# One transpose and one small transfer for a row of maxima, maxima moved behind and between, and a reordered first front

## What is computed

```python
k_sh = head_rmsnorm(kvf[..., :D]); v_sh = kvf[..., D:2 * D]
c_all = jnp.cumsum(log_sigmoid(kvf[..., 2 * D:] + kv_f_bias), axis=1)
q = head_rmsnorm(proj[..., :D]); z = proj[..., D:]
logits = (q @ k.T) * HEAD_DIM ** -0.5 + c_q - c_k      # causal, per head
out = h + ((softmax(logits) @ v) * silu(z)) @ w_out
```

## Time and profile before

| what | us |
|---|---|
| median of 3 runs | 1886.25 (1883.72 to 1886.79) |
| the profiled execution | 1883.0 |
| its span | 1880.9 |
| PE busy in it | 1812.6 (96%) |
| DVE, ACT, POOL busy | 965.2, 945.8, 465.6 |

### The profile page before, as it was taken

The page is one execution under the profiler, slowest core; times in us unless marked ns, Lnnn a source line. Parts: engine busy times, 40 slices in busy tenths (PEclk is TensorE's granted clock), DMA queues, the critical chain, the costliest instruction groups (busy, mean ns, idle before and its releaser), DMA issues.

```text
span 1880.9 us, 55776 instructions
## 1 busy us (share of the span) xinstructions
PE 1812.6 (96%) x24247; PEld 1578.4 (84%) x24247; DVE 965.2 (51%) x1864; ACT 945.8 (50%) x1721; POOL 465.6 (25%) x464
## 2 busy tenths in 40 slices
PE   6899999999999999999899999999999999999998
PEld 5798989889898999899798888888888888887676
DVE  6456666666666666666533833443443344334421
ACT  6555454555545464555423645555455555554621
POOL 3323242423324242332500411212121212111000
PEclk9999999999999999999999999999999999999999
DMA  7101010100101010010342200111110111111334
GB/s 251 34 9 45 9 53 9 42 17 21 41 9 51 9 53 9 28 31 9 105 136 76 88 23 23 29 29 30 34 35 24 40 28 30 29 29 30 100 104 136
DMA packets 105362, 88.78 MB, mean 47 GB/s; under 512 B 4065, under 2 KB 96852, under 8 KB 104996
## 3 DMA queue, kind: packets, MB, share of 16 engines
q1 hardware_dynamic: 99400, 65.87, 12.1%
q0 software_dynamic: 2864, 12.34, 2.1%
q10 hardware_dynamic: 2860, 7.02, 1.1%
HBM read 64.43 MB, written 20.80 MB: 45 GB/s over the span
## 4 chain that ended last, share of the span: by engine, by line
PE 87%; DVE 5%; ACT 4%; issue 2%; POOL 1%; DMA 1%; SPq 0%; ACTq 0%; DVEq 0%
PE ps L2115 8%; PE ps L2752 7%; PE ps L2645 6%; PE ps L2116 6%; PE ps L2117 6%; PE ps L2646 6%; PE ps L2647 6%; PE ps L2028 3%; PE ps L2030 3%; PE ps L2029 3%; PE ps L2207 3%; PE ps L2226 3%; PE ps L2721 2%; PE ps L2694 2%; PE ps L2724 2%
## 5 line engine op out<-in xcount | busy, mean ns | idle before, releaser
L2115 PE MATMUL ps<-xh,wh 128*128 128x258 f32 (+1 forms) x1008 | 315.0, 313 | 3.6 <-ACT arena L1190 2.2
L2116 PE MATMUL ps<-xh,wl 128*128 128x258 f32 (+1 forms) x1008 | 286.3, 284 | 0.0
L2117 PE MATMUL ps<-xl,wh 128*128 128x258 f32 (+1 forms) x1008 | 286.2, 284 | 0.0
L2645 PE MATMUL ps<-xh,wh 128*128 128x348 f32 x744 | 253.7, 341 | 4.6 <-ACT arena_b L1446 3.8
L2646 PE MATMUL ps<-xh,wl 128*128 128x348 f32 x744 | 239.1, 321 | 0.0
L2647 PE MATMUL ps<-xl,wh 128*128 128x348 f32 x744 | 239.0, 321 | 0.0
L1973 DVE TENSOR_REDUCE arena_b<-ps 128x1 f32<-128x144 f32 (+4 forms) x224 | 106.5, 506 | 200.5 <-PE ps L2698 180.3
L2115 PEld LDWEIGHTS ps<-xh,wh 128*128 128x128 f32 x1008 | 190.3, 189 | 16.2 <-ACT arena L1190 3.6
L2116 PEld LDWEIGHTS ps<-xh,wl 128*128 128x128 f32 x1008 | 190.8, 189 | 2.0
L2117 PEld LDWEIGHTS ps<-xl,wh 128*128 128x128 f32 x1008 | 190.1, 189 | 0.0
L1149 ACT ACTIVATE arena<-ps,pp 128x257 f32<-128x257 f32 (+1 forms) x128 | 61.1, 478 | 225.6 <-PE ps L2117 225.6
(11 more groups left out here) (320 smaller groups left out, 4538.8 us busy)
## 6 DMA issues: line engine op xcount, KB each, us to landing
wr<-in_w_in SPq DMA_DIRECT2D x33, 512.0 KB, 4.5
wr<-in_kv_w SPq DMA_DIRECT2D x16, 512.0 KB, 4.0
wr<-in_b_w_in SPq DMA_DIRECT2D x16, 512.0 KB, 4.0
arena<-xt_scr SPq DMA_DIRECT2D x8, 522.0 KB, 4.4
xt_scr<-arena POOLq DMA_DIRECT2D x1, 4176.0 KB, 13.5
wr<-in_w_out SPq DMA_DIRECT2D x8, 512.0 KB, 4.2
ob_scr<-arena_b POOLq DMA_DIRECT2D x16, 256.0 KB, 2.9
wr<-in_b_w_out SPq DMA_DIRECT2D x8, 512.0 KB, 5.2
```

Of the source, the lines that this page charges most:

```text
L2115: pe.matmul(bank, wh[:, j, k, :], xh[:, k, t], start=(k == 0), stop=False)
L2116: pe.matmul(bank, wl[:, j, k, :], xh[:, k, t], start=False, stop=False)
L2117: mm = pe.matmul(bank, wh[:, j, k, :], xl[:, k, t], start=False, stop=(k == KO - 1))
L2645: pe.matmul(bank[:, 0:SEG], wh[:, slot, k, :], xh[:, k, t], start=(k == 0), stop=False)
```

## The change

- `maxrow`: PE makes one transpose of all 8 columns of `mcol` into 8 partitions of one bank; ACT copies it negated to a new tile `m_neg` (8 x 128), waits for that copy (`m_neg`), and issues a DMA that writes it as 1,024 values of one partition of `qb2`. The first scores wait for the DMA's semaphore, the users of the bank for `m_neg` alone.
- `order`: a new list `mid[g]` stands between `scores` of group g+1 and `weighted` of group g. Projection pieces are not interrupted any more; two maxima stand behind a piece, and up to two in `mid`.
- `first_round` has `maxrow` 0 ahead of the last half piece of z, and the last pair has `maxrow` 1 ahead of its `bo` step in fill 7.
- `FRONT_ONLY` begins with the k and v steps; r is whole ahead of `kks`. The copy and the shift of the third low-rank piece move into the step `low`.

```diff
@@ order @@
-                    fill[2] = m(2) + proj(0, 1, *m(2))
-                    fill[3] = m(2) + proj(0, 2, *m(2))
-                    fill[4] = ([("sumsq", 0, i) for i in range(3)] + [("den", 1), ("rsq", 0)] + proj(1, 0, *m(2)) + m(1))
-                    fill[5] = m(2) + proj(1, 1, *m(1)) + [("norm", 0)]
+                    fill[2] = proj(0, 1) + m(2)
+                    mid[2] = m(2)
+                    fill[3] = proj(0, 2) + m(2)
+                    mid[3] = m(2)
+                    fill[4] = [("sumsq", 0, i) for i in range(3)] + [("den", 1), ("rsq", 0)] + proj(1, 0) + m(2)
+                    mid[4] = m(1)
+                    fill[5] = proj(1, 1) + [("norm", 0)] + m(2)
+                    mid[5] = m(1)
...
-                    fill[7] = [("bo", 0, 2), ("maxrow", 1)]
+                    fill[7] = [("maxrow", 1), ("bo", 0, 2)]
...
-                fill[3] = [("vrow", 0, 0), ("vrow", 0, 1)] + m(2) + proj(3, 0, *m(2))
-                fill[4] = m(2) + proj(3, 1, *m(2)) + [("gated", 0)]
-                fill[5] = m(2) + [("proj", 3, 2, 0)] + m(2)
-                fill[6] = m(2) + [("wsplit",)]
+                fill[3] = [("vrow", 0, 0), ("vrow", 0, 1)] + proj(3, 0) + m(2)
+                mid[3] = m(2)
+                fill[4] = proj(3, 1) + [("gated", 0)] + m(2)
+                mid[4] = m(2)
+                fill[5] = [("proj", 3, 2, 0)] + m(2)
+                mid[5] = m(2)
+                fill[6] = [("wsplit",)] + m(2)
...
-                steps += [("weighted", e, g)]
+                steps += mid[g] + [("weighted", e, g)]
@@ first_round @@
-            return steps + maxima[10:] + z[5:] + [("maxrow", 0)]
+            return steps + maxima[10:] + [("maxrow", 0)] + z[5:]
@@ FRONT_ONLY @@
-        FRONT_ONLY = ([("low",), ("decay",), ("first", 3)] + FRONT_IN[0][1:] + sum(FRONT_IN[1:5], []) + FRONT_IN[5][:2]
-                      + [("rsqrt",)] + FRONT_IN[5][2:] + FRONT_IN[6])
+        FRONT_ONLY = ([("k", 2), ("v", 2), ("low",), ("decay",), ("first", 3), ("exps",), ("kraw",), ("tables",), ("r", 0),
+                       ("r", 1), ("r", 2), ("kks",)] + FRONT_IN[5][:2] + [("rsqrt",)] + FRONT_IN[5][2:] + FRONT_IN[6])
@@ ACT, ahead of the list and in low @@
-            act.wait_ge(S.lora_part, 3)
-            act.activation(mut_lo[:, 2 * SEG + 1:], G[0][:, 2, :], ACT.Copy, scale=param(C_LORA)).then_inc(S.mu_done, 1)
+            act.sem_inc(S.mu_done, 1)
...
+                        if begin:
+                            act.wait_ge(S.lora_part, 3)
+                            act.activation(mut_lo[:, 2 * SEG + 1:], G[0][:, 2, :], ACT.Copy, scale=param(C_LORA))\
+                                .then_inc(S.lora_mu, 1)
@@ DVE, the same @@
+                        if begin:
+                            dve.wait_ge(S.lora_mu, 3)
+                            dve.scalar_tensor_tensor(seg3(lo)[:, 2, :], G[0][:, 2, :], param(C_NLORA), lora_mut[:, 2, :],
+                                                     ALU.mult, ALU.add).then_inc(S.hi_part, 1)
@@ ACT, maxrow @@
-                        for a in range(2):
-                            act.wait_ge(S.m_row_done, 4 * q_ + 2 * e + a + 1)
-                            act.activation(qb2[e][HD:HD + 1, META + a * 512:META + (a + 1) * 512], ps[0:1, B_SM[a], :],
-                                           ACT.Copy, scale=-1.0).then_inc(S.m_row, 1)
+                        n_ = 2 * q_ + e
+                        act.wait_ge(S.m_row_done, n_ + 1)
+                        if n_:
+                            act.wait_ge(S.m_row, 16 * n_)
+                        act.activation(m_neg[:, :], ps[0:KO, B_SM[0], 0:P], ACT.Copy, scale=-1.0).then_inc(S.m_neg, 1)
+                        act.wait_ge(S.m_neg, n_ + 1)
+                        act.dma_start(f32(qb2[e][HD:HD + 1, META:T]), f32(m_neg[:, :])).then_inc(S.m_row, 16)
@@ PE, maxrow and scores @@
-                        for a in range(2):
-                            for t in range(4):
-                                mm = pe.transpose(ps[0:1, B_SM[a], t * P:(t + 1) * P], mcol[:, 4 * a + t:4 * a + t + 1],
-                                                  ident[:, :])
-                            mm.then_inc(S.m_row_done, 1)
+                        pe.transpose(ps[0:KO, B_SM[0], 0:P], mcol, ident[:, :]).then_inc(S.m_row_done, 1)
...
-                                pe.wait_ge(S.m_row, 4 * p + 2 * e + 2)
+                                pe.wait_ge(S.m_row, 16 * (2 * p + e + 1))
```

More of the change, by code:

```diff
@@ L208, in __init__ @@
         self.m_row = sem("m_row")
+        self.m_neg = sem("m_neg")
         self.st_done = sem("st_done")
@@ L262, in build @@
         params = sb("params", [P, NCOLS])
+        m_neg = sb("m_neg", [KO, P], F32R)
         pp = sb("pp", [P, NQ])
@@ L457, in m @@
                 return [next(maxima) for _ in range(n)]
-            fill = [[] for _ in GROUPS]
+            fill, mid = [[] for _ in GROUPS], [[] for _ in GROUPS]
             if e == 0:
@@ L1197, in round_act_a @@
                         if begin:
-                            act.wait_ge(S.shifted, 1)
+                            act.wait_ge(S.hi_part, 3)
                             act.activation(lo[0:LORA, SEG_T[0][1]:], lo[0:LORA, SEG_T[0][1]:], ACT.Tanh)\
@@ L1640, in _ @@
             dve.scalar_tensor_tensor(seg3(lo)[:, 1, :], G[0][:, 1, :], param(C_NLORA), lora_mut[:, 1, :], ALU.mult, ALU.add)
-            dve.wait_ge(S.mu_done, 1)
-            dve.scalar_tensor_tensor(seg3(lo)[:, 2, :], G[0][:, 2, :], param(C_NLORA), lora_mut[:, 2, :], ALU.mult,
-                                     ALU.add).then_inc(S.shifted, 1)
+            dve.sem_inc(S.shifted, 1)
             def split_row(r, k):
@@ L2600, in _ @@
                     if first and i < 2:
-                        pe.wait_ge(S.hi_part, i + 3)
+                        pe.wait_ge(S.hi_part, i + 4)
                     elif i == 0 or first:
@@ L2656, in round_pe @@
                             elif not first:
-                                pe.wait_ge(S.m_row, 4 * p + 4)
+                                pe.wait_ge(S.m_neg, 2 * p + 2)
                             elif j == 0:
@@ L2685, in round_pe @@
                             if not first:
-                                pe.wait_ge(S.m_row, 4 * q_ + 2 * e)
+                                pe.wait_ge(S.m_neg, 2 * q_ + e)
                         elif i >= 2:
@@ L2734, in round_pe @@
                             if m:
-                                pe.wait_ge(S.m_row, 4 * KO)
+                                pe.wait_ge(S.m_neg, 2 * KO)
                             else:
```

## The result

The change made the kernel slower: median 1903.97 us against 1886.47 us before (6 runs each), a ratio of 1.009 with a 95% interval of 1.0074 to 1.0106. The forecast was 1875 us. The profiled execution took 1899.9 us, 16.9 more than the one before.

What follows compares the result with a forecast made beforehand. PE, busy 96% of the span, was taken as the bound; -12.2 + 3.3 + 1.1 - 3.0 = -10.8 us from the median of 1886.25 gave 1875.4, stated as 1875. Range 1868 to 1883, leaving out rivals 2 and 3.

Steps and rivals of the forecast that it cites:

- Transposes, -12.2 us: In `maxrow`, one transpose replaces eight: 0.76 us saved 16 times, all on the path.
- The row's way: From transpose to first scores by copy and DMA: issue at +0.65, row there at +2.45, needed at +2.9; stall 0.
- The two bounds of 2.6 and 4.0 us: Slower landings of the row's DMA, from two other loads: row there at +3.25 or +4.65, stalls 0.35 or 1.75.
- The collision: At `maxrow`, SP's weight load comes 0.6 to 0.8 us earlier and overlaps the row's traffic; a few tenths lost, inside cover.
- Rival 2: Before the first scores, the row queues behind the weight load or lands at 4.0 us: +17 us, 1892; chance 0.07.
- Uncovered wait, +3.3 us: Second half of a pair: maxima no longer cover the z piece's wait for the v rows; 0.47 us over 7 pairs.
- Shortest group, +1.1 us: Maxima pairs around the shortest scores wait for DVE's reductions of two PSUM banks: 0.15 us over 7 pairs.
- First front, -3.0 us: Before the first mask: k and v steps earlier, r whole, z starts near 60.9 and ends at 66.0 instead of 69.0.
- Rivals 3 and 4: Maxima wait for DVE at 49 places, 1886, chance 0.09; the front gives nothing because of later waits, 1878, chance 0.1.

Runs made afterwards that it cites:

- row_only: Kernel before with only the new `maxrow` (one transpose, copy, DMA), maxima in their old places within `order`; 1875.58 us, ratio 0.9958.
- split_only: Changed kernel with only ACT's split of the next k weights moved behind the row of maxima; 1877.84 us, ratio 0.9951.
- cover_only: Changed kernel with only the first two maxima of a pair's second half put ahead of the z piece again; 1896.22 us, ratio 1.0049.
- wait_filled: cover_only with six repeats of a product, thrown away, ahead of PE's wait for head 0's row; 1884.77 us, ratio 0.9998.
- order_only: Kernel before with only the new fills and `mid`, the old `maxrow` kept; 1890.01 us, ratio 1.0029.

## Why the prediction was wrong

- *Transposes, -12.2 us*: right in mechanism, a tenth too large: 1.36 us per pair instead of 1.53. The whole of row_only is -9.6 us, with 1.5 us of waits in it.
- *The row's way*: the issue at +0.61 against +0.65, the landing alone at 1.8 us, as taken: in row_only and split_only PE uses the row 2.16 us after the issue without a wait, and at head 1 of the last pair, where its cover is shortest, at 1.84. The two bounds of 2.6 and 4.0 us were not needed for a transfer by itself.
- *The collision, "Eight small packets between 1024 should lose a few tenths, inside the cover"*: this is the step that failed. I had worked out that the load would come 0.6 to 0.8 us earlier against the row; it did (0.97 us behind the transpose before, 0.34 now). What I priced wrongly was the meeting. The row's packets did not go between the load's but behind them, which costs the row about 2 us: seven landings of 3.7 to 4.6 us after the issue instead of 1.8, +11.6 us of waits. Rival 2 had this mechanism and place, and its 1.75 us for one wait was near the 1.66 measured; but it counted nine places and more, 17 us, and seven came about: the first round has no load near its row, and head 1 of the last pair has none either. It got 0.07, and its time of 1892 was still 12 us short.
- The rule of the Trainium skill that I set beside rival 2 ("DMA: Bandwidth & Descriptors", the section on queues, rings and completion order: a DMA engine takes turns between queues packet by packet) was taken to make it a few tenths. In the trace the row's packets do not take turns with the load's: issued 0.27 us behind it, they ran at its end and the row landed in 3.8 us; 0.37 us ahead of it, PE had the row in 2.2, with one exception of 2.7. The section's packet holds several descriptors, typically 9 to 17 and at most 64; the load has 1,024 pieces of 512 B, an estimated 64 on each of 16 engines. So "packet by packet" leaves room for a wait of a whole load, which "a few tenths" left out. That the load was one packet on each engine is not shown, and the row in the middle of the load (0.16 us ahead) speaks against it.
- *The clock*: missing. I had the two gaps' own lengths in the sum or in the rivals and assumed the full level around them, though the trace before shows the level falling behind gaps in the front and in the last pair. Between cover_only and wait_filled it is 11.4 us, in the changed kernel 13 in the windows from 1180 to 1700 us alone. That is the largest single error, and why even rival 2 fell short.
- *Uncovered wait, +3.3 us*: right. 0.45 us per pair, 0.47 forecast. *Shortest group, +1.1 us*: 0.04 per pair instead of 0.15; nothing.
- *First front, -3.0 us*: -2.2 measured. The interval of its ratio reaches from -4.0 to -0.4 us, so the term stands. Its working has a slip: by its own rates, 24 products from 60.9 with the slow level until 65.2 end at 66.3, not 66.0, which gives -2.7.
- Rivals 3 and 4 did not come about: L2711 waits 3.9 us for DVE in the whole span against 5.1 before, and the front's gain stayed. (The 4.9 us before all lie in the last pair, none in the first round.)

Summed up again with what was measured: 1886.5 - 9.5 for the transposes - 2.2 + 3.3 + 11.6 + 13 gives 1902.7, against 1904.0. Part of that match is luck: the 13 us leave out the lower clock outside 1180 to 1700 us, and the terms count seven pairs, not all. The sum is better tested on the stretch of 649.2 us: -9.5 + 3.3 + 11.6, and 15.4 for ten falls of the clock of 1.54 us each (the price of one is worked out at the end), give +20.8 against 21.7 measured.

## What to carry to other kernels

- In a kernel bound by PE, price a wait by what it leaves in its neighbourhood: a gap of 1.1 to 1.7 us, harmless by itself, cost as much again through the clock here. Filling it with products that are thrown away was worth 11.4 us here; removing it is better.
- Here a small transfer with 2 us of cover was late whenever a large one was issued just ahead of it, or less than 0.2 us behind. Look at every queue's issues within 1 us of it after the change, not before it; here the remedy was to put ACT's copy, from which the load follows by way of GpSimd and SP, behind the row.
- Measure the parts alone when a change has several: -2.2, -9.6 and +4.9 us were each within 2.6 us of their forecast, and only their meeting gave +17.5.

## What the runs showed of the hardware that was not expected

- The issue of the row's DMA occupies ACT's queue for 0.63 to 0.66 us (8 rows of 512 B into one partition; the first two of a run took 1.26 and 0.7), against 0.23 us for the 8.2 KB load of two rows.
- The race is decided by 0.3 us or so: the row's DMA issued 0.37 us ahead of the load lands in time, 0.16 us ahead it already lands late (3.45 us), and 0.27 us behind it at 3.8 to 4.6 (3.7 in the one case of 0.49).
- In order_only the same gap of 1.1 us pulled the clock down in three pairs in a row and in none of the four others. Each pair with a fall took 91.9 us, each without 90.36: 1.54 us for a stretch of about 3.4 us at the lower level. What decides whether it falls is left open here.
